# A two-block transformer forward pass on one core: the beta product as one stationary, modulated rows from the fifth block of the last up product, and weights' halves between the turned pairs

## What is computed

```python
def gated_deltanet(xn, w_in, conv_w, A_log, dt_bias, out_norm_w, w_out):
    proj = xn @ w_in                                  # qkv 3072 columns, z 1024, then 8 beta and 8 gate columns
    qkv = jax.nn.silu(causal_dwconv(proj[..., :A_CONV_WIDTH], conv_w))
    beta = jax.nn.sigmoid(b_raw)
    g = -jnp.exp(A_log) * jax.nn.softplus(a_raw + dt_bias)
    o = chunk_gated_delta_rule(q, k, v, beta, g)      # uses the cumulative sums of g in chunks, and their differences
    o = rmsnorm(o, out_norm_w) * jax.nn.silu(z)
    return o @ w_out

def conv_ffn(xn, w_up, conv_w, conv_b, w_down):       # up: 1024 -> 2 x 2816, down: 2816 -> 1024
    h = causal_dwconv(xn @ w_up, conv_w) + conv_b
    return (jax.nn.silu(gate) * val) @ w_down

# second block, last part
mod = c_act @ w_mod + b_mod                           # sh1, sc1, g1, sh2, sc2, g2
h2 = rmsnorm(x, norm2_g) * (1 + sc2) + sh2            # sh2: one number for each channel
x = x + g2 * (jnp.square(jax.nn.relu(h2 @ w_ff1)) @ w_ff2)
```

## Time and profile before

| | |
|---|---|
| device time, median of 3 runs | 1042.59 us (1040.06 to 1043.23) |
| span of the profiled execution | 1037.3 us |
| median less span (what lies outside the span) | 5.3 us |
| PE busy | 998.8 us, 96% |
| DVE busy | 848.9 us, 82% |
| ACT busy | 608.4 us, 59% |
| POOL busy | 102.2 us, 10% |
| mean granted TensorE clock | 0.994 |
| DMA | 193.09 MB, mean 186 GB/s |

### The profile page before, as it was taken

How to read it: one execution, slowest core, us unless ns; L and a number is a source line. 1 busy time by engine, 2 the same in 40 slices (tenths; PEclk the granted TensorE clock), 3 DMA queues, 4 the chain that set the end, 5 groups by cost and what they waited for, 6 DMA issues and landing times.

```text
span 1037.3 us, 20795 instructions
## 1 busy us (share of the span) xinstructions
PE 998.8 (96%) x7662; PEld 926.7 (89%) x7662; DVE 848.9 (82%) x1566; ACT 608.4 (59%) x1056; POOL 102.2 (10%) x115
## 2 busy tenths in 40 slices
PE   6999999999999999999899999999998899999996
PEld 6999898999998889988899998898777799998884
DVE  5899978798889979887898999867788876668856
ACT  6687534666666464574676666456364565545443
POOL 1014522000000000001100001001200210000001
PEclk9999999999999999999999999999999999999998
DMA  9674323687776868837786657834412158766852
GB/s 290 178 223 135 103 64 101 204 228 219 222 210 218 287 175 256 278 100 262 252 237 197 186 185 251 283 95 130 152 62 82 41 152 245 193 188 219 278 152 115
DMA packets 216194, 193.09 MB, mean 186 GB/s; under 512 B 6032, under 2 KB 193568, under 8 KB 216000
## 3 DMA queue, kind: packets, MB, share of 16 engines
q1 hardware_dynamic: 206560, 158.09, 51.4%
q0 software_dynamic: 9136, 33.51, 9.5%
q10 hardware_dynamic: 432, 0.61, 0.2%
HBM read 191.14 MB, written 1.06 MB: 185 GB/s over the span
## 4 chain that ended last, share of the span: by engine, by line
PE 84%; DVE 8%; ACT 4%; DMA 2%; issue 1%; POOL 1%; POOLq 0%; ACTq 0%; DVEq 0%
PE ps L606 23%; PE ps L607 22%; PE ps L608 22%; PE ps L1315 3%; PE ps L1316 3%; PE ps L1314 3%; DVE wL L2187 2%; DMA modw<-in_w_mod_t 1%; PE ps L887 1%; PE ps L874 1%; ACT wH L1361 1%; PE ps L1144 1%; DVE cv L2209 1%; PE ps L829 1%; PE ps L783 1%
## 5 line engine op out<-in xcount | busy, mean ns | idle before, releaser
L1361 ACT ACTIVATE wH<-raw 128x1024 fp32r<-128x1024 f32 x298 | 312.9, 1061 | 254.9 <-PE ps L608 190.7
L2187 DVE TENSOR_TENSOR wL<-raw,wH 128x1024 fp32r<-128x1024 f32 x298 | 357.7, 1225 | 59.5 <-ACT wH L1361 58.8
L606 PE MATMUL ps<-yH,wH 128*128 128x256 f32 x704 | 195.7, 278 | 3.7 <-DVE wL L2187 3.6
L607 PE MATMUL ps<-yL,wH 128*128 128x256 f32 x704 | 194.5, 276 | 0.0
L608 PE MATMUL ps<-yH,wL 128*128 128x256 f32 x704 | 194.5, 276 | 0.0
L606 PEld LDWEIGHTS ps<-yH,wH 128*128 128x128 f32 x704 | 132.2, 188 | 4.7 <-DVE wL L2187 1.5
L607 PEld LDWEIGHTS ps<-yL,wH 128*128 128x128 f32 x704 | 132.2, 188 | 0.1
L608 PEld LDWEIGHTS ps<-yH,wL 128*128 128x128 f32 x704 | 132.2, 188 | 0.0
L606 PE MATMUL ps<-wH,aH 128*128 128x512 f32 (+1 forms) x308 | 119.4, 388 | 0.0
L608 PE MATMUL ps<-wH,aL 128*128 128x512 f32 (+1 forms) x308 | 119.0, 386 | 0.0
L607 PE MATMUL ps<-wL,aH 128*128 128x512 f32 (+1 forms) x308 | 119.0, 386 | 0.0
(11 more groups left out here) (430 smaller groups left out, 2178.2 us busy)
## 6 DMA issues: line engine op xcount, KB each, us to landing
raw<-in_f_w_up SPq DMA_DIRECT2D x88, 512.0 KB, 4.9
raw<-in_w_ff SPq DMA_DIRECT2D x64, 512.0 KB, 4.5
modw<-in_w_mod_t POOLq DMA_DIRECT2D x48, 512.0 KB, 5.5
raw<-in_f_w_down SPq DMA_DIRECT2D x44, 512.0 KB, 4.6
raw<-in_a_w_in SPq DMA_DIRECT2D x32, 512.0 KB, 4.9
raw<-in_w_in SPq DMA_DIRECT2D x22, 512.0 KB, 4.3
raw<-in_w_kv SPq DMA_DIRECT2D x16, 512.0 KB, 5.2
raw<-in_a_w_out SPq DMA_DIRECT2D x8, 512.0 KB, 3.4
```

The source lines that it names most:

```text
L606: mm(o, l[0], r[0], start=first, stop=False, skip_group_check=check)
L607: mm(o, l[0], r[1], start=False, stop=False, skip_group_check=check)
L1361: fn(slot(wH, c), raw[:, c % RAW], ACT.Copy).then_inc(hi_done, 1)
L2187: return tt(o, x, hi.bitcast(F32), ALU.subtract)
```

## The change

1. **Gates.** `ba2` holds baH and baL side by side (32 columns): two matmuls for each k in place of three, 16 in all. 32 rows are copied and turned, and `gates_in` adds the two halves. The 16 gate row products go. Instead, DVE copies g into every 32nd-column group of `g_cols` (`gates(2)`, at block 7), PE multiplies it with the triangle behind block 9 (L1272, one 128x128 fp32 product), DVE spreads the result over four column groups with a mask (`gate_rows`, L2483, 128x512, after the convolution of block 10), and PE's `gate_sums` waits for that and adds up with four products of 32 rows by 512 columns (L814).
2. **Modulated rows.** Blocks 0 to 3 of ff1 stay. From block 4 on (`SHIFTED_UP = 4`, 12 blocks) the operand is h2 itself, mt = (nH + nL) x row scale (POOL, two adds and two multiplications of 128x1024) plus the shift, split by ACT (`modulated_hi`, 8 x 128x256) and DVE (`modulated_lo`, 8 x 128x256) in turn 2. PE waits for both ahead of block 4 and then issues plain blocks of 256 columns. ACT evacuates them with relu at once; DVE has only the weights' halves and the square.
3. **Joins of wo_a and wo_b.** The halves of one unit stand between the pairs 2 and 3, those of the other behind the last pair's statistics. In wo_b's join the sums go (3, 1, 0, 0) instead of (2, 2, 1, 0); the fifth, the context squares of ACT and the three context steps of DVE move into up1 (behind its two head blocks, and at blocks 18, 19, 20). In up0 and up1 the first `ahead` stands before `row_scale`. On POOL, mod_fetch up to 46 stands ahead of the wait for `y_ready` and of `row_f1` and `ctx_in`.

```diff
+                pe.wait_ge(g_rows_dve, 1)
                 for g in range(4):
-                    for x in range(4):
-                        n = 4 * g + x
-                        last = mm(ps[AUX + g][:, x * P:(x + 1) * P], sm[:, 10, n:n + 1].broadcast_to([P, P]), K_["tri"],
-                                  start=True, stop=True)
-                    last.then_inc(row_pe, 1)
+                    r = slice(32 * g, 32 * g + 32)
+                    mm(ps[AUX + g][:], K_["ones"][r], g_rows[r].rearrange("p y n -> p (y n)"),
+                       start=True, stop=True).then_inc(row_pe, 1)
...
-                        last = three(ps[AUX][0:16, 0:SEQ], [baH[:, k], baL[:, k]], [y[:, k] for y in X], k == 0, k == KD - 1)
+                        for f in range(2):
+                            last = mm(ps[AUX][0:32, 0:SEQ], ba2[:, k], X[f][:, k], start=k == 0 and f == 0, stop=k == KD - 1 and f == 1)
                     last.then_inc(ba_done, 1)
+
+                if j == 9:
+                    pe.wait_ge(g_cols_dve, 1)
+                    mm(ps[AUX + 2][:, 0:P], g_cols[:], K_["tri"], start=True, stop=True).then_inc(g_cols_pe, 1)
...
+                def modulated(i, j):
+                    b = bank("ff1", i, j)
+                    for f in range(2):
+                        w = weights(i, U("ff1") + 2 * j + f)
+                        for k in range(KD):
+                            last = three(b[:, f * SEQ:(f + 1) * SEQ], [y[:, k] for y in w], [y[:, k] for y in X],
+                                         k == 0, k == KD - 1)
+                        last.then_inc(unit_done, 1)
+                turns(pe, BLOCKS["ff1"][1], body, between=lambda: pe.wait_ge(mt_ready, 2))
...
-                    if j == 3:
-                        for b in (2, 3):
-                            turned_pair(n, n, b, AUX + b, gain, yH)
+                    if j < 3:
+                        ahead(0, U(name) + 2 * j)
+                    else:
+                        turned_pair(n, n, 2, AUX + 2, gain, yH)
+                        hi(0, 8, U(name) + 2 * j + SPLIT)
+                        turned_pair(n, n, 3, AUX + 3, gain, yH)
                         part(3)
-                    ahead(0, U(name) + 2 * j)
+                        hi(0, 8, U(name) + 2 * j + SPLIT + 1)
...
-                if l == 1:
+
+                def context_squares():
                     act.wait_ge(late_in, 32)
-                    squares("ctx", ctx_in, xvc[:].rearrange("p (t k) n -> p t (k n)", t=TT))
+                    squares("ctx", ctx_in, ctx_sq)
...
+                turns(act, BLOCKS[up][1], body, between=context_squares if l == 1 else None, before_last=first_tiles(down_))
...
+            def modulated_hi():
+
+                for part in range(2):
+                    act.wait_ge(mt_rows, part + 1)
+                    for k in range(4 * part, 4 * part + 4):
+                        last = fn(xH[:, k], mt[:, k], ACT.Identity, bias=modc[:, 24 + k, 0:1])
+                    last.then_inc(mt_hi, 1)
...
+                n = STAGED["ff1"] + j
+                if j >= SHIFTED_UP:
+                    act.wait_ge(unit_done, i * 8 + (U("ff1") + 2 * j + 2))
+                    act.wait_ge(unstaged, i * 4 + (n - 1))
+                    fn(stage[:, n % 2].rearrange("p a b -> p (a b)"), ps[(BANK["ff1"] + j) % 4][:],
+                       ACT.Relu).then_inc(bank_free, 1)
+                    ahead(i, U("ff1") + 2 * j)
+                    return
                 ahead(i, U("ff1") + 2 * j)
-                n = STAGED["ff1"] + j
+                if j == 2:
+                    modulated_hi()
...
-            mod_fetch(38)
+            mod_fetch(46)
 
             pool.wait_ge(y_ready, BAND_Y + BAND_PAIRS)
             pool.dma_start(row_f1[:], a["rows_c"][:, 0:1024].partition_broadcast(P).rearrange("p a n -> p (a n)")).then_inc(late_in, 16)
             pool.dma_start(ctx_in[:], a["ctx_2"].rearrange("o (t p) d -> p (o t) d", p=P)).then_inc(late_in, 16)
-            mod_fetch(46)
+            norm("f1")
             pool.wait_ge(mod_used, mod_before(MOD_LATE))
             pool.dma_start(tb[:], a["tables"]).then_inc(tables_in, 16)
             pool.dma_start(rows_c[:], a["rows_c"][:, 1024:1664].partition_broadcast(P).rearrange("p a n -> p (a n)")).then_inc(tables_in, 16)
-            norm("f1")
+            mod_fetch(46, 33)
...
             norm("n2")
+            for part in range(2):
+                c = slice(4 * part, 4 * part + 4)
+                pool.wait_ge(x_ready, READY["n2"] + 2 * part + 2)
+                ptt(mt[:, c], nH[:, c, 0:SEQ].bitcast(F32), nL[:, c].bitcast(F32), ALU.add).then_inc(mt_sum, 1)
+            pool.wait_ge(r_done, r_order.index("ff1") + 1)
+            for part in range(2):
+                c = slice(4 * part, 4 * part + 4)
+                pool.wait_ge(mt_sum, part + 1)
+                ptt(mt[:, c], mt[:, c], four_of(rcol), ALU.mult).then_inc(mt_rows, 1)
...
-                        for b in (2, 3):
-                            turned_pair(n, b, AUX + b, gain, yH, yL)
+                        turned_pair(n, 2, AUX + 2, gain, yH, yL)
+                        lo(0, 8, U(name) + 2 * j + SPLIT)
+                        turned_pair(n, 3, AUX + 3, gain, yH, yL)
                         mean_square(n, 4)
-                        lo(0, 8, U(name) + 2 * j + SPLIT)
+                        lo(0, 8, U(name) + 2 * j + SPLIT + 1)
...
+                dve.wait_ge(g_dve, 4)
+                dve.wait_ge(g_zero, 1)
+                nc.vector.tensor_copy(g_cols[:].rearrange("p (g y) -> p g y", y=32)[:, :, 0:4],
+                                      sm[:, 10, 0:16].rearrange("p (g x) -> p g x", x=4)).then_inc(g_cols_dve, 1)
+
+            def gate_rows():
+
+                dve.wait_ge(g_cols_pe, 1)
+                tt(g_rows[:], rep(ps[AUX + 2][:, 0:P], 4), bc(K_["pick"], P), ALU.mult).then_inc(g_rows_dve, 1)
...
+                if j == BLOCKS["qkv"][1] - 2:
+                    gate_rows()
...
+            def context_rows(part):
+
+                if part == 0:
+                    modulation()
+                    dve.wait_ge(sq_done, 2 * STAT["ctx"] + 2)
+                    ts(msq[:], ssq[:], 1.0 / D, EPS, ALU.mult, ALU.add).then_inc(ms_done, 1)
+                elif part < 3:
+                    t = part - 1
+                    dve.wait_ge(rstd_done, STAT["ctx"] + 1)
+                    ts(ctx_in[:, t], ctx_in[:, t], rstd[:, t:t + 1], None, ALU.mult).then_inc(xn_done, 1)
...
+                    if first:
+                        ahead(i, U(up) + 2 * j)
+                        row_scale(up)
...
+                    if l == 1 and isinstance(i, int) and j >= F_TILES - 4:
+                        context_rows(j - F_TILES + 4)
+                turns(dve, BLOCKS[up][1], body, st, 2 * F_TAPS - 3, between=(lambda: mod_sums(1)) if l == 1 else None,
...
-            added("wo_b", "f1", lambda k: col("f_norm1", k), after=lambda j: mod_sums((2, 2, 1, 0)[j]))
+            added("wo_b", "f1", lambda k: col("f_norm1", k), after=lambda j: mod_sums((3, 1, 0, 0)[j]))
...
+            def modulated_lo():
+
+                for part in range(2):
+                    dve.wait_ge(mt_hi, part + 1)
+                    for k in range(4 * part, 4 * part + 4):
+                        last = stt(xL[:, k], mt[:, k], modc[:, 24 + k, 0:1], xH[:, k].bitcast(F32), ALU.add, ALU.subtract)
+                    last.then_inc(mt_ready, 1)
...
+                if j == 2:
+                    modulated_lo()
```

61 lines of the change are left out of this document (41 added, 20 removed).

## The result

Over 20 executions of each, the changed kernel took 1045.07 us (1040.14 to 1049.67) and the one before 1040.49 (1037.93 to 1048.70). The ratio on record is 1.0032, with a 95% interval of 1.0017 to 1.0047: some 3.3 us **slower** (the two medians differ by 4.6 us, inside that interval). I had forecast 3.0 us faster. The time of before from which the sum was made, 1042.59, was the median of three; twenty give 1040.49, so the three alone put the forecast 2 us too high. I had also read 5.3 us as what lies outside the span. In the runs that list both, the time is 1.8 to 1.9 us above the span (2.4 in one), so the profiled execution of before took some 1039.1 us and was not a median one.

A forecast was written before the change was run, and what follows sets the result against it. PE was taken as the bound, so only fewer matmul columns or PE waits count. From 1042.6 us, -0.7 (part 1) + 0.4 (part 2) + 0.5 and 2.8 (joins) made 3.0 gained: 1039.6 us, range 1037.4 to 1043.2.

The forecast's parts named there:

- Part 1: Beta and gates: 0.7 us lost (0.1 to 3.2), with PE idle 4.6 us ahead of the gate sums.
- the array works on four groups of rows side by side: Gate sums: the four 32-row products take 1.06 us if all run side by side, 3.57 if in turn.
- The beta product: Beta product: 8 matmuls fewer at 0.113 us each, 0.9 us less on PE.
- DVE's next half starts where it did, so the DVE chain through the delta stage is not late: Behind the gate sums: DVE's next half still starts at 81.2; a later DVE wait swallows 0.7 of PE's 1.4 us.
- Part 2: Modulated rows in ff1: 3.2 us less on PE minus 2.8 of wait, 0.4 gained (-0.9 to 1.1).
- The wait ahead of block 4: ff1: PE waits 2.8 us for the modulated rows, 2.1 without POOL's cost to DVE plus 0.7 for it.
- The two additions run in a stretch where DVE waits for PE: ff1: POOL's two additions add nothing to PE's wait; only its two multiplications delay DVE, by about 0.7 us.
- The upper bound in my text: ff1, ahead of block 4: if POOL and DVE fully exclude each other, the wait is 4.1 us, part 2 losing 0.9.
- The blocks' gain: ff1: twelve blocks at 5.43 us and not 5.70 take 3.2 us off PE.
- The same number, two thirds of them 258 columns wide: ff1 against up1: 48 matmuls a block in both; the wider columns were taken to make 5.70 us of 5.43.
- Part 3: Joins: 0.5 us gained at wo_a and 2.8 at wo_b (1.0 to 3.1) by removing PE's waits for DVE.
- The clock rival: Gate sums and ff1 waits: each brings half clock, 3.4 us together, so 0.4 slower, 1043.0 us; chance 0.20.

The follow-up runs named there:

- beta_only: The kernel before with only the beta product as one stationary of 32 columns, without g_cols, g_rows and the four products; 0.9973 of before, 2.8 us faster.
- a_alone: The kernel before with only the beta and gates change (item 1 of the diff); 1.0011 of before (0.9997 to 1.0024).
- b_nopool: The kernel before with only the modulated rows, made without POOL's four instructions (no nL, no row scale); 1.0022 of before (1.0004 to 1.0040).
- c_alone: The kernel before with only the joins change (item 3 of the diff); 0.9987 of before (0.9971 to 1.0003).
- the one run made to keep the clock: The changed kernel with useless products keeping PE busy in its two new long waits; 1.0027 of before (1.0006 to 1.0049).

## Why the prediction was wrong

**What bounds the kernel**: right as far as it went. Each difference is one of PE's waits, its matmuls, their start-to-start time, or its clock; the last two were not in the forecast's sum.

**Part 1** (0.7 lost): measured 1.1 (-0.3 to 2.5). The wait (4.6 against 4.5) was right, though both of its ends came 0.9 us later than forecast, and so was that the array works on four groups of rows side by side: 1.14 us at full clock against 1.06, but 2.09 in the changed kernel, at half clock. Two terms failed. The beta product was worth 2.8 us (1.5 to 4.2), not 0.9, likely by a rarer fall of the clock. And the step "DVE's next half starts where it did, so the DVE chain through the delta stage is not late" compared with before and not with what the beta product alone would give: measured against beta_only the gate rows cost 3.9 us (2.0 to 5.9), of which taking PE's wait away returned 0.5, not told from nothing. Why they cost that stays open. One candidate is DVE's work in a stage that it paces. The other is the clock, whose median is 0.992 in a_alone and 0.996 in beta_only, an estimated 4 us. That part 1 as a whole came out near its forecast is luck: by the medians the beta product gave 1.9 us more and the gate rows cost 2.3 more than the sum had (3.9 against 1.6).

**Part 2** (0.4 gained): measured 4 lost (1.6 to 6.4). This is the step that turned the sign. The wait ahead of block 4 (2.8) was nearly right (3.0). Missed was the wait of 1.5 us ahead of block 3. The step that failed is "The two additions run in a stretch where DVE waits for PE": they fell on DVE's scaling of the diagonals, took 4.2 us more of it than before, pushed its halves behind them, and the multiplications met the next ones with no slack left. I had put 0.7 us of DVE's delay down to POOL; b_nopool put it at 2.3 us of PE's waits. The upper bound in my text was 4.1 us of wait; the two waits sum to 4.5. The rule of "SBUF — State Buffer" of the Trainium skill (section on the two separate sides) that I had weighed and not taken is borne out by the two halves, each with two SBUF inputs, that took 4.22 us beside the multiplications' 4.77. The scaling has one such input, so the rule as I told it does not cover it; that it took 4.76 us beside POOL's 4.74 is what the rows show.
The blocks' gain (3.2) was in the sum as certain. It is 3.1 where the blocks ran 5.44 us apart, in the three profiles where the clock had fallen ahead of them, at a price of 1.4 to 2.3 us, and 0.5 in the two where they ran 5.66 apart. "The same number, two thirds of them 258 columns wide" took the whole difference of the earlier trace rows for one of width; blocks of 256 columns ran at either pace.

**Part 3** (3.3 gained): measured 1.3 (-0.3 to 3.0). In the joins the forecast was met: the profile of c_alone, 0.4 us ahead at 431, is 4.5 ahead at 511. What failed is what the text left out: that the tables, rows and three tiles of w_mod, 3 MB, would be issued together at 515, since their wait is on the sum that moved into up1. The price was a wait of 1.3 to 2.8 us, in two of the four profiles that show it with a fall of the clock. With the loads put back the part is worth 2.3 (0.6 to 4.1).

**The rivals.** The clock rival named both places and the sign. The clock fell in all five executions profiled with a wait of 4.4 to 4.6 us (three at the gate sums, two ahead of the product of `g_cols`); at ff1's wait of 3.0 in two of four. Over all executions the changed kernel's median clock is 0.991 against 0.995, an estimated 4 us at most, about what was lost; the rival had 3.4. But the forecast's other 3.0 us did not come either, so the clock is not the only thing that failed. By the parts, the loss is mostly part 2 (4.0 us) and the gate rows (3.9), against 2.8 and 1.3 gained by the beta product and the joins. How each splits into waits and clock is not shown, since the one run made to keep the clock kept half of it.

## What to carry to other kernels

When a load waits for a step that moves, list what else then goes out with it, and into which stretch of weights' loads. A fair baseline for a part is the change without it: the gate rows looked cheap against before and cost 3.9 us against the beta product alone. Before two POOL instructions on wide SBUF operands are put beside DVE, look for what DVE has to do there, short instructions too: here one of 0.58 us became 4.76. Compare mean granted clocks over all executions before a cause is read from a trace. With differences of 0.3%, profile each kernel more than once before its two traces are subtracted.
